# Two attention stages of a decoder trunk: a fixed owner for each copy out of PSUM, results turned unit by unit, and a compressed branch woven between the units

## What is computed

```
u = h @ w_in                      # pooled channels, q, k, v
q, k = rope(q), rope(k)
y_b = softmax(mask(q k^T / 8)) v  # 12 heads
x = x + concat(y_a, y_b) @ w_out_ab
```

```
k_cmp = gelu(blocks(kc) @ k_w1) @ k_w2        # 15 per group, same for v
o_cmp = softmax(mask(q_unrotated k_cmp^T / 8)) v_cmp
y = g0*o_cmp + g1*o_sel + g2*o_win            # sigmoid gates per head
x = x + y @ w_out_c
```

## Time and profile before

| | |
|---|---|
| median of 3 runs | 1708.44 us (1707.26, 1708.44, 1720.1) |
| profiled execution, its own time | 1704.51 us |
| its span, mean granted clock | 1702.8 us, 0.959 |
| PE busy | 1591.8 us, 93% |
| PEld / DVE / ACT / POOL busy | 1316.2 / 1255.9 / 1071.2 / 23.4 us |
| HBM read | 432.49 MB |

### The profile page before, as it was taken

The page is one execution under the profiler, slowest core; times in us unless marked ns, Lnnn a source line. Parts: engine busy times, 40 slices in busy tenths (PEclk is TensorE's granted clock), DMA queues, the critical chain, the costliest instruction groups (busy, mean ns, idle before and its releaser), DMA issues.

```text
span 1702.8 us, 21759 instructions
## 1 busy us (share of the span) xinstructions
PE 1591.8 (93%) x7746; PEld 1316.2 (77%) x7747; DVE 1255.9 (74%) x1364; ACT 1071.2 (63%) x1268; POOL 23.4 (1%) x52
## 2 busy tenths in 40 slices
PE   7988689999998887799999999999999999999997
PEld 5767568887786766688888888888888888888885
DVE  4544345554535653799998998998998998998996
ACT  4452444444423443588777877877877877887874
POOL 5000000000000000000000000000000000000000
PEclk9997799999998997899999999999999999999998
DMA  9510136467450032599999999999999999999960
GB/s 357 206 37 0 50 99 212 157 208 290 151 184 12 1 130 100 191 387 373 338 371 364 343 357 376 344 354 344 370 362 344 368 360 339 376 352 345 373 248 25
DMA packets 199809, 434.16 MB, mean 255 GB/s; under 512 B 6906, under 2 KB 35668, under 8 KB 199764
## 3 DMA queue, kind: packets, MB, share of 16 engines
q1 hardware_dynamic: 197184, 432.22, 70.2%
q0 software_dynamic: 288, 1.05, 0.2%
q10 hardware_dynamic: 2292, 0.28, 0.1%
HBM read 432.49 MB, written 1.05 MB: 255 GB/s over the span
## 4 chain that ended last, share of the span: by engine, by line
PE 91%; DVE 5%; ACT 3%; issue 1%; DMA 0%; ACTq 0%; DVEq 0%
PE ps L1045 18%; PE ps L1050 18%; PE ps L1047 18%; PE ps L628 8%; PE ps L631 7%; PE ps L634 7%; PE ps L739 3%; PE ps L1016 2%; PE ps L679 2%; PE ps L1071 1%; PE ps L703 1%; DVE f_w_lo L1504 1%; PE ps L915 1%; ACT f_w_hi L1149 1%; DVE hT_lo L1516 1%
## 5 line engine op out<-in xcount | busy, mean ns | idle before, releaser
L1961 DVE TENSOR_TENSOR w_lo<-ring,w_hi 128x1024 fp32r<-128x1024 f32 x672 | 813.2, 1224 | 55.4 <-ACT w_hi L1429 15.6
L1429 ACT ACTIVATE w_hi<-ring 128x1024 fp32r<-128x1024 f32 x672 | 712.0, 1062 | 184.0 <-PE ps L1050 184.0
L1045 PE MATMUL ps<-w_hi,x_hi 128*128 128x512 f32 x896 | 353.2, 394 | 2.4 <-DVE x_lo L1967 2.4
L1047 PE MATMUL ps<-w_hi,x_lo 128*128 128x512 f32 x896 | 349.5, 390 | 0.0
L1504 DVE TENSOR_TENSOR f_w_lo<-ring,f_w_hi 128x1024 fp32r<-128x1024 f32 (+1 forms) x139 | 169.0, 1225 | 155.3 <-ACT f_w_hi L1149 154.7
L1050 PE MATMUL ps<-w_lo,x_hi 128*128 128x512 f32 x896 | 276.3, 389 | 0.0
L1149 ACT ACTIVATE f_w_hi<-ring 128x1024 fp32r<-128x1024 f32 (+1 forms) x139 | 145.2, 1056 | 174.4 <-PE ps L634 165.4
L628 PE MATMUL ps<-f_w_hi,hT_hi 128*128 128x512 f32 (+2 forms) x480 | 188.2, 396 | 23.8 <-DVE hT_lo L1516 10.3
L1045 PEld LDWEIGHTS ps<-w_hi,x_hi 128*128 128x128 f32 x896 | 168.3, 188 | 36.6 <-issue 2.6
L1050 PEld LDWEIGHTS ps<-w_lo,x_hi 128*128 128x128 f32 x896 | 168.1, 188 | 36.4 <-DVE w_lo L1961 0.3
L1047 PEld LDWEIGHTS ps<-w_hi,x_lo 128*128 128x128 f32 x896 | 168.3, 188 | 34.0
(11 more groups left out here) (243 smaller groups left out, 1283.7 us busy)
## 6 DMA issues: line engine op xcount, KB each, us to landing
ring<-in_moe_w_gate SPq DMA_DIRECT2D x56, 2048.0 KB, 8.5
ring<-in_moe_w_up SPq DMA_DIRECT2D x56, 2048.0 KB, 8.5
ring<-in_moe_w_down SPq DMA_DIRECT2D x56, 2048.0 KB, 8.0
ring<-in_ffn_w_gate SPq DMA_DIRECT2D x11, 1024.0 KB, 5.4
ring<-in_ffn_w_up SPq DMA_DIRECT2D x11, 1024.0 KB, 8.0
ring<-in_ffn_w_down SPq DMA_DIRECT2D x11, 1024.0 KB, 5.4
ring<-in_w_in_ab SPq DMA_DIRECT2D x5, 2048.0 KB, 17.4
ring<-in_w_in_c SPq DMA_DIRECT2D x5, 2048.0 KB, 12.6
```

Of the source, the lines that this page charges most:

```text
L1045: pe.matmul(ps[:, bnk, :], hi, w_h, start=first_ and (bnk != part.open), stop=False, skip_group_check=True)
L1047: pe.matmul(ps[:, bnk, :], lo, w_h, start=False, stop=False, skip_group_check=True)
L1429: sc_.activation(w_hi[:, high_e.k % STAGES, :], raw(slot, q), ACT.Copy).then_inc(hi_ready, 1)
L1961: ve.tensor_tensor(w_lo[:, st, :], raw(slot, q), w_hi[:, st, :].bitcast(F32), ALU.subtract).then_inc(lo_ready, 1)
```

## The change

1. `by_dve` replaces the counters: in a causal unit VectorE copies the block (1, 0), the second of three; in cross-attention the ones with kc = 1, the second and the fourth.
2. In MoBA the results of a unit are turned by `y_turn` (two column blocks, four transposes into bank 5) as soon as VectorE has them; ScalarE (`y_high`) and VectorE (`y_low`) make the halves. `project` takes a list of what each quarter waits for and a function that runs after the first quarter: the turn of the last unit.
3. In NSA the hidden layer is cut in four pieces (`hidden`), the turned queries and keys, the second layer (`compressed`), the compressed scores, their turn and weighted sum become pieces between the units. They use bank 5 and its semaphores, the hidden layer banks 6 and 7. Keys are laid out block-diagonally: `kcmpT` [128, 2, 2, 15] is zero except for the group's own half, so that one matmul of 30 columns over 128 rows gives two groups' scores. For p = 0 the results of the first branch (br = 0) are written to `u` without an addition and the compressed result is added to them later; for p = 1 it is copied there first, as before. The results are turned in four steps by `y_turn`.
4. ScalarE's query copies stand between the two halves of a unit's exponentials. The second Gelu comes after unit 1's exponentials. `branch` moves to the columns of the unrotated compressed keys in `u`.

```diff
+        def by_dve(causal_, tt, kc):
+            return (tt, kc) == (1, 0) if causal_ else kc == 1
+        def y_rows(m):
+            k = m // 2 * 4 + m % 2
+            return slice(k, k + 3, 2)
 # TensorE
-            def project(n, fresh=False):
+            def project(n, fresh=False, needs=None, after_first=None):
...
+                    if needs is not None:
+                        pe.wait_ge(*needs[q])
...
+                    if q == 0 and after_first is not None:
+                        after_first()
+            def bank_free(full, done):
                 if t.value(full):
                     pe.wait_ge(done, t.value(full))
+                if full is dve_turn_full and y_turn.stand < t.value(xT_full):
+                    turned_stand()
+                    y_turn.stand = t.value(xT_full)
+            def y_turn(blocks):
+                pe.wait_ge(heads_ready, t.next(heads_ready))
+                bank_free(dve_turn_full, dve_turn_done)
+                for j, blk in enumerate(blocks):
+                    mm = pe.transpose(ps[:, 5, j * P:(j + 1) * P], blk, ident[:, :])
+                mm.then_inc(xT_full, 1)
+                t.next(xT_full)
...
             moba_scores(2)
             moba_weighted(0)
             turn_probs(1, probs[1], True)
+            moba_y(0)
             moba_weighted(1)
             turn_probs(2, probs[0], True)
+            moba_y(1)
             moba_weighted(2)
-            heads(u[:, :, QA0:QA0 + MOBA], MOBA // P)
-            pe.wait_ge(yT_lo_ready, 1)
-            turned_stand()
-            for j in range(2):
-                project(512)
             pe.wait_ge(probs_ready, 2 * MOBA_UNITS)
+            y = t.value(xT_full)
+            project(512, needs=[(yT_lo_ready, 1)] + [(hT_lo_ready, y - 1 + i) for i in range(MOBA_UNITS)],
+                    after_first=lambda: moba_y(2))
+            project(512)
...
+            def cmp_scores():
+                bank_free(dve_turn_full, dve_turn_done)
+                for tt in range(TT):
+                    for p in range(2):
+                        for hd in range(4):
+                            at = tt * 240 + p * 120
+                            mm = pe.matmul(ps[:, 5, at:at + 120].rearrange("p (b c) -> p b c", b=2)[:, :, hd * NCMP:(hd + 1) * NCMP],
+                                           qcT[:, 2 * p + hd // 2, hd % 2, tt * P:(tt + 1) * P], kcmpT[:, p, :, :],
+                                           start=True, stop=True, skip_group_check=True)
...
+            hidden(0, 0)
+            hidden(0, 1)
+            pe.wait_ge(roped, 2)
+            nsa_turn_q(0)
+            nsa_turn_k(0)
+            pe.wait_ge(act_turn_done, t.value(act_turn_full))
+            pe.wait_ge(dve_turn_done, t.value(dve_turn_full))
+            nsa_scores(0)
+            nsa_turn_q(1)
...
+            hidden(1, 0)
+            nsa_scores(1)
+            nsa_turn_k(1)
...
+            hidden(1, 1)
+            nsa_probs_turn(0)
...
+            nsa_scores(2)
+            nsa_turn_q(2)
...
+            compressed()
+            nsa_weighted(0)
+            nsa_probs_turn(1)
+            nsa_scores(3)
+            nsa_turn_q(3)
...
+            cmp_scores()
+            nsa_weighted(1)
+            nsa_probs_turn(2)
...
+            nsa_scores(4)
+            nsa_weighted(2)
+            nsa_probs_turn(3)
+            nsa_scores(5)
+            cmp_turn()
+            nsa_weighted(3)
+            nsa_probs_turn(4)
...
+            nsa_scores(6)
+            cmp_weighted()
+            nsa_weighted(4)
+            nsa_probs_turn(5)
+            nsa_scores(7)
+            nsa_y(0)
+            nsa_weighted(5)
+            nsa_probs_turn(6)
+            nsa_y(1)
+            nsa_weighted(6)
+            nsa_probs_turn(7)
+            nsa_y(2)
+            nsa_weighted(7)
...
+                    after_first=lambda: nsa_y(3))
 # ScalarE
+            gelu(0)
+            nsa_q(0)
+            nsa_exps(0, lambda: nsa_q(1))
+            nsa_exps(1)
+            gelu(1)
+            turn_probs(pT, True)
+            nsa_exps(2, lambda: nsa_q(2))
+            turn_probs(pT, True)
+            nsa_exps(3, lambda: nsa_q(3))
+            turn_probs(pT, True)
+            sc_.wait_ge(cmp_shifted, 1)
+            sc_.activation(ec[:, :, :, :], sc[:, :, :, :], ACT.Exp).then_inc(cmp_exp, 1)
+            nsa_exps(4)
...
+            nsa_exps(7, lambda: y_high(y_rows(0)))
 # VectorE, MoBA
             tops(1, True)
+            ve.wait_ge(yT_hi_ready, 1)
+            ve.tensor_tensor(hT_lo[:, 0:2, :], u[:, 0:2, 0:S], hT_hi[:, 0:2, :].bitcast(F32), ALU.subtract).then_inc(yT_lo_ready, 1)
             turn_probs(pT, True)
             tops(2, True)
             moba_result(0)
+            heads_stand()
             turn_probs(pT, True)
+            y_low(slice(2, 4))
             moba_result(1)
...
 # VectorE, NSA
+            tops(7, True)
+            cmp_shift()
+            nsa_result(1)
+            turn_probs(pT, True)
+            tops(8, True)
+            nsa_result(2)
+            turn_probs(pT, True)
+            cmp_weigh()
+            tops(9, True)
```

More of the change, by code:

```diff
@@ L947, in _, with hidden @@
-            mm.then_inc(cmp_full, 1)
-            pe.wait_ge(cmp_kv_ready, 2)
+            def hidden(v, hh):
+                if hh == 0:
+                    hidden.w = ring[:, unit(MID_FIRST + len(IN_C) + v), :].rearrange("p (k n) -> p k n", k=16)
+                for j in range(16):
+                    mm = pe.matmul(ps[:, 6 + v, hh * 60:(hh + 1) * 60], hidden.w[:, j, hh * P:(hh + 1) * P],
+                                   X[:, v, j // 8, :, j // 8:j // 8 + NCMP, j % 8], start=(j == 0), stop=(j == 15))
+                    if hh == j == 0:
+                        mm.then_inc(weights_used, 1)
+                if hh:
+                    mm.then_inc(mlp_full, 1)
@@ L1188, in take, with exps @@
                 ins.then_inc(acc_free[0], 1)
-            def exps(a, buf, is_causal):
+            def exps(a, buf, is_causal, between=None):
                 for tt in range(TT):
+                    if tt and between is not None:
+                        between()
                     keys = P if is_causal and tt == 0 else S
@@ L1400, in _ @@
+            high(MOE_FIRST - 4, 3)
             arrived(MOE_FIRST - 3)
@@ L1734, in _ @@
             heads_stand()
[L1735 to L1739 removed]
+            low(7, 1)
+            low(7, 2)
+            y_low(slice(6, 8))
+            low(7, 3)
             low(8, 0)
@@ L1885, in _, with cmp_result @@
-            heads_stand()
-            heads(0, KD)
-            for q in range(1, 4):
-                low(MOE_FIRST - 4, q)
+                weighted(dst, gate_of, fresh=(p == 0 and br == 0))
+                if br and p:
+                    heads_stand()
+            def cmp_result():
+                for p in range(2):
+                    for tt in range(TT):
+                        ve.wait_ge(pv_full, t.next(pv_full))
+                        at = u[:, tt, p * 512:(p + 1) * 512]
+                        if p:
+                            ins = ve.tensor_copy(at, ps[:, 6 + tt, :])
+                        else:
+                            ins = ve.tensor_tensor(at, at, ps[:, 6 + tt, :], ALU.add)
+                        ins.then_inc(pv_done, 1)
+                ve.wait_ge(pv_done, t.value(pv_full))
+                ve.nop().then_inc(heads_ready, 2)
@@ new lines, in _ @@
+            tops(9, True)
+            nsa_result(3)
+            turn_probs(pT, True)
+            tops(10, True)
+            cmp_result()
+            nsa_result(4)
+            turn_probs(pT, True)
+            tops(11, True)
+            y_low(y_rows(0))
+            nsa_result(5)
+            turn_probs(pT, True)
+            y_low(y_rows(1))
+            nsa_result(6)
+            turn_probs(pT, True)
+            y_low(y_rows(2))
+            ve.wait_ge(act_turn_full, 36)
+            low(MOE_FIRST - 4, 0)
@@ L1889, in _ @@
+            nsa_result(7)
+            low(MOE_FIRST - 4, 1)
+            low(MOE_FIRST - 4, 2)
+            y_low(y_rows(3))
+            low(MOE_FIRST - 4, 3)
             low(MOE_FIRST - 3, 0)
```

307 lines of the change are left out of this document (149 added, 158 removed).

## The result

The changed kernel took 1685.45 us (median; 1684.51 to 1686.26) beside 1708.32 for the kernel before (median of four): a ratio of 0.985 with a 95% interval of 0.9807 to 0.9894, or 23 us saved where 24 were forecast. A second comparison of the same kernel, shown among the experiments, gave 1678.98 (1668.74 to 1686.0), a ratio of 0.982 (0.9775 to 0.9864). The profiled execution has a span of 1682.8 us at a mean granted clock of 0.961; before it was 1702.8 at 0.959.

The account below looks back on a forecast made before the run. TensorE's chain bounds the kernel, with recoverable loss in MoBA and NSA attention from idle gaps and half clock. Savings 5.4 + 16.7 + 1.5 = 23.6, say 24, forecast a 1684 us median; range 1674 to 1698.

Parts of the forecast that it names:

- Copy order: Causal units and cross-attentions: every unit 6.84 us, saving 1.05 per unit of the second kind; 1.5 in both cross-attentions together.
- MoBA: MoBA attention: results turned per unit close the gap before the projection, saving 5.4 us with copy order, clock unchanged.
- NSA: NSA with its compressed branch: 107.7 us becomes 85.6 at full clock; 16.7 us saved after the clock allowance.
- ScalarE's two table loads: ScalarE around NSA's second Gelu: two added loads at 1.28 us each, costed at nothing, 3 if uncovered.
- clock term: NSA stage: 5 us given back for half clock: 1.9 a sum, 1.6 turns, 1.5 a spell after compressed scores.
- the first NSA scores: Sign in NSA: the first scores come some 9 us after the hidden layer's start if the forecast is right.
- Block-diagonal keys: NSA's compressed scores: 32 matmuls over 128 rows take 3.6 us, 1 us less than the 64 short ones.
- Later stages keep their length: Stages after attention: length unchanged, because their weights already wait in the ring.
- (a): Attention stages: waits return or half clock persists; NSA saves 8, total 15, about 1694 us; chance 0.16 with (d).
- (b): Expert loop: weight loads set its pace and absorb the earlier start; time stays at 1707 us; chance 0.04.
- (c): Hidden layer or first units: clock falls and stays low through mixed narrow work; about 1728 us; chance 0.03.
- (d): VectorE's queue: an early wait holds each unit's copy, 0.7 us a unit, about 1692 us; chance 0.16 with (a).

Follow-up runs that it names:

- e1: The kernel before with the fixed copy order alone; 1713.04 us, ratio 0.9957.
- e2: The kernel before with the fixed copy order and MoBA's results turned per unit, NSA otherwise as before; 1706.84 us, ratio 0.9937.
- e6: The changed kernel with four extra matmuls of 512 columns, read by nothing, ahead of the hidden layer; 1677.18 us, ratio 0.9792.
- e3: The changed kernel with NSA's results again turned together behind the last unit, ahead of the output projection; 1677.97 us, ratio 0.9858.
- e4: The changed kernel with block-diagonal keys undone: 64 matmuls of 15 columns over 64 rows; 1678.36 us, ratio 0.9843.
- e7: The changed kernel with the 48 gate columns ahead of the last 512 in NSA's input projection; 1676.04 us, ratio 0.9814.
- e10: The changed kernel itself, unaltered, run once more on one chip beside e3, e4 and e7; 1678.98 us, ratio 0.982.
- e13: The kernel before with the fixed copy order and four unread matmuls of 512 columns ahead of its hidden layer; 1698.49 us, ratio 0.9937.
- e5: The changed kernel with only the hidden layer's first quarter ahead of the first scores, the rest and both Gelus later; 1676.02 us, ratio 0.9779.
- e12b: The changed kernel with the 48 columns first and five unread 512-column matmuls in TensorE's wait ahead of the gather; 1674.59 us, ratio 0.9797.

## Why the prediction was right, and where it was not

**The total was right, with a smaller share of structure in it than the sum had.** 24 were forecast; the medians give 23 and 31, the profiles 20, the adjusted spans 16 to 18. That the total came so near is partly luck, because errors of 6 us cancel. Against the sum's 23.6, MoBA gave 6.0 more than its term and NSA 6.6 less; the stretches with the two cross-attentions gave 4.3 instead of 1.5, and the later stages that were to keep their length took back 5.8, which leaves 20. The clock is most of each.

**Copy order.** A steady unit is now 548.43 - 541.50 = 6.93 us, then 7.28 with a turn of 0.45 in it; 6.84 was forecast for every unit. Four NSA units gave 4.1 (e1), forecast 4.2. In the cross-attention the exponentials to the sum were 9.74 us and are 9.03: 0.7 each, forecast 0.8. MoBA's share was 0.5 instead of 1.05. These add up to 6, e1's adjusted span has 3.0; the missing 3 us I can't place.

**MoBA.** Forecast 5.4, measured 11.4, of which 0.42 x (21 - 3) = 7.6 is clock and 3.7 structure. The step "for MoBA I leave the clock as it was" is the one that failed: part of the 5.7 us gap was itself half clock, and with the results turned unit by unit the last two units run at 1.00, in this and in nine other profiles (see e2). What in that arrangement keeps the clock up isn't isolated. The window answers the earlier trace rows:

```profile
132.00:136.00 4.00, 3.52 (x30) 2.95 (x29) 1.59 (x4) 1.32 (x3) 0.00 (x0) 1.00 0.00 0
```

**NSA.** The list of TensorE's work at full clock was 85.6 us. The changed stage less its clock share is 85.3, and e6, with 3 us at half clock, took 86.1: the terms hold, and ScalarE's two table loads cost nothing visible. ScalarE's row around the first of them has no gap on either side of the load:

```profile
514.64 1.56 ACT L1299 ACTIVATE att<-ps,nmax 128x256 f32<-128x256 f32 x4 [0.78 <-DVE nmax L1713]
516.22 1.28 ACT L1485 ACT_TABLE_LOAD   x1
517.52 0.57 ACT L1485 ACTIVATE kvm<-ps 128x480 f32<-128x480 f32 x1
```

So the drain that the Trainium skill ("ScalarE: Activation LUTs", What ACT_TABLE_LOAD costs) adds doesn't show here. What failed is the size of the saving, 16.7 against 10.1, through the **clock term**: the 107.7 us of before held 22 us at half clock, and the full-clock list set against them counted all of that as saved; I gave back 5 us, but the changed stage held 29 us at half clock, which is 12. By structure the stage saved 98.7 - 85.3 = 13.4. The time at half clock also lay elsewhere than I had put it. The end of the stage, where I had put 3.5, runs at full clock (2.79 at 580.61); the loss is in the hidden layer's first half, costed at 7.2 and measured at 13.75. The profile of before had it at full clock; e1 and e2, with the same instructions up to there but for the copy order and MoBA, had it at half (27.4 us). I took one execution's row for the kernel's. One sign failed with it: the first NSA scores came 16.4 us behind the hidden layer's start instead of 9 (9.1 in e3, whose hidden layer was at full clock). The spell behind the compressed scores was there (4.68 at 534.16), but lasted 6.8 us, about 2.9 us of cost where 1.5 was put.

**Block-diagonal keys.** 3.6 forecast, 3.65 measured; but they win nothing over the old form at full clock, not 1 us (e4). The old form's 0.073 us each held time at half clock; at full clock it is 0.059, just half of the 0.114 of the new one.

**Later stages keep their length** failed by 5.8 us in these profiles (the table's two negative rows), nearly all of it clock and none of it weights: finer windows give 32 us at half clock instead of 26 in the first of them, and 20 instead of 14 between the router and the experts' first activation, together about 5 us at 0.42.

**Rivals.** (a) came true in its clock half. Its condition was 12 us more at half clock than the allowance of 5 us covers; the allowance covers 12 us, 29 were measured, so 17 more. NSA's 10.1 is nearer its 8 than to 16.7. Its exposed copies didn't come, and MoBA's gain kept the total away from 1694. (b) is out, since the expert loop begins earlier by what was won. (c) is out as a whole, though its mechanism, a low clock held through narrow work, is real (e1, e2). (d) is out, the waits for copies between the units being 0.34 to 0.59.

## What to carry to other kernels

Before costing a stage from one profile, look at the granted clock of each of its rows, and keep a sum at full clock apart from a clock term; here the first held within 1 us and the second was off by more than twice. When medians of variants disagree with their edits, adjust each execution by its time at half clock before drawing conclusions. Place narrow matmuls behind wide ones with care: what comes last ahead of a long narrow stretch can decide its clock, and swapping two pieces made the time steadier (e7's six spans lie within 6.6 us, e10's within 17.3), though the changed kernel's shortest executions, 1667.0 and 1667.2, were shorter than any of e7's.

## What the runs showed of the hardware

In the long pieces, the 60-column matmuls kept the clock level that they met: 128 of them took 27.40 us at half clock in e1 and 14.44 at full clock in e13, with the same neighbours but for four wide matmuls. It isn't without exception: in e5 the return came 1 us into a piece of 32 of them that followed scores.

Ahead of the hidden layer the fall came at one of two places, about 3 us into the 48-column piece or at its end, in kernels with identical instructions up to there. The clock was at half when the hidden layer began only after the early fall, and not when wide matmuls stood between (e13). What tips it is open.

Within 512-column work the clock came back each time that it was low there: in the projection in e7 (at 477.5, 7.7 us into it) and in inserted matmuls in e13 and e12b. It can fall there too: in e12b it was low from 671.1 to 674.5 in the experts' first matmuls, behind a wait of 2.4 us. In the profile of before and in e3 to e6 it also came back during the four turns ahead of the hidden layer, so wide work isn't necessary.

Two half-height matmuls of 15 columns cost about the same as one full-height matmul of 30: 2 x 58.6 ns against 114.
